# Half of the w_out projection set into attention, its norm split in two, and the norm between two blocks done by row tile

## The reference

```
first block:
  proj = rmsnorm(x) @ w_in                       # 1024 x 2560, cut into q, k, v, u, vg
  sb   = stick_breaking_attention(q, k, v)       # 8 heads of 64, causal
  sg   = gelu(u) * (W_spatial . rmsnorm(gelu(vg)) + b)      # "gated" unit, 512 wide
  h    = x + concat(rmsnorm(sb), rmsnorm(sg)) @ w_out       # 1024 x 1024
  h    = h + moe(rmsnorm(h))     # 4 groups x 8 experts of width 512, 2 experts per token
  y    = rmsnorm(h) * g_final
second block:
  z    = rmsnorm(y) @ w_in_2 + b                 # 1024 x 7168
  u    = causal depthwise convolution, 31 taps (conv_a), layer norm, silu, product
  v    = short convolution, RG-LRU scan, product; gated sum; projection w_o
  x    = y + m @ w_o; x = x + relu(rmsnorm(x) @ w_1)^2 @ w_2;  rmsnorm
```

## Time and profile before

| what | value |
|---|---|
| time, median of 3 runs | 1077.96 us (1077.39 to 1079.14) |
| the profiled execution's own time | 1080.09 us |
| its span | 1078.6 us |
| TensorE busy | 896.8 us (83%) |
| VectorE busy | 526.9 us (49%) |
| ScalarE busy | 344.6 us (32%) |
| POOL busy | 133.4 us (12%) |
| DMA, mean over the span | 278 GB/s, 299.98 MB |
| the chain that ended last | PE 52%, DMA 29%, DVE 14%, ACT 2% |

### The profile page before, as it was taken

The page is one execution under the profiler, slowest core; times in us unless marked ns, Lnnn a source line. Parts: engine busy times, 40 slices in busy tenths (PEclk is TensorE's granted clock), DMA queues, the critical chain, the costliest instruction groups (busy, mean ns, idle before and its releaser), DMA issues.

```text
span 1078.6 us, 18062 instructions
## 1 busy us (share of the span) xinstructions
PE 896.8 (83%) x7891; PEld 724.1 (67%) x7891; DVE 526.9 (49%) x845; ACT 344.6 (32%) x463; POOL 133.4 (12%) x67
## 2 busy tenths in 40 slices
PE   8998988966475746475565899999999989999997
PEld 8987875533243424242342599689999989988986
DVE  4644554222131212112021769999997857635542
ACT  5624221100000001000000734557756446443531
POOL 1032400000000000000001288603210000000000
PEclk9998999888787868778688899999999999999999
DMA  9870748999999999999999645325568444546420
GB/s 343 260 300 2 300 168 371 426 426 427 426 428 428 428 428 430 428 428 430 428 428 420 198 162 191 117 93 171 168 211 283 173 170 166 207 157 218 173 78 39
DMA packets 86727, 299.98 MB, mean 278 GB/s; under 512 B 12381, under 2 KB 50701, under 8 KB 74253
## 3 DMA queue, kind: packets, MB, share of 16 engines
q1 hardware_dynamic: 86525, 299.13, 70.7%
q10 hardware_dynamic: 144, 0.00, 0.0%
HBM read 298.07 MB, written 1.05 MB: 277 GB/s over the span
## 4 chain that ended last, share of the span: by engine, by line
PE 52%; DMA 29%; DVE 14%; ACT 2%; issue 2%; SPq 1%; DVEq 0%
DMA mem<-in_w_up 25%; PE PS L1772 12%; PE PS L1773 12%; PE PS L1774 12%; PE PS L1954 8%; DVE PS L1547 6%; PE PS L1967 3%; DMA mem<-in_w_down 3%; DMA mem<-in_w_in 1%; DVE PS L1572 1%; PE PS L1940 1%; DMA mem<-in_w 1%; PE PS L1980 1%; PE PS L1746 1%; DVE PS L1568 1%
## 5 line engine op out<-in xcount | busy, mean ns | idle before, releaser
L1954 PE MATMUL PS<-mem 128*32 128x256 f32 x2048 | 156.6, 473 | 136.0 <-DMA mem<-in_w_up 135.4
L1954 PEld LDWEIGHTS PS<-mem 128*32 128x32 f32 x2048 | 83.6, 136 | 210.6 <-issue 184.6
L1774 PE MATMUL PS<-HT_hi,ring_rest 128*128 128x256 f32 x752 | 212.8, 283 | 0.0
L1774 PEld LDWEIGHTS PS<-HT_hi,ring_rest 128*128 128x128 f32 x752 | 143.9, 191 | 0.0
L1328 DVE TENSOR_TENSOR mem<-mem,PS 128x128 f32<-128x128 f32 x32 | 12.1, 379 | 261.2 <-ACT mem L809 261.2
L1772 PE MATMUL PS<-HT_hi,z_hi 128*128 128x256 f32 x440 | 124.9, 284 | 2.3 <-DVE ring_rest L1522 2.3
L1773 PE MATMUL PS<-HT_rest,z_hi 128*128 128x256 f32 x440 | 124.5, 283 | 0.0
L653 POOL TENSOR_TENSOR ring_rest<-mem,z_hi 128x2048 fp32r<-128x2048 f32 x19 | 87.6, 4622 | 95.1 <-DVE ring_rest L1522 55.9
L1685 DVE TENSOR_TENSOR ring_rest<-mem,mlp_hi 128x4096 fp32r<-128x4096 f32 x16 | 70.8, 4424 | 57.7 <-ACT mlp_hi L1027 57.7
L809 ACT ACTIVATE mem<-PS 128x128 f32<-128x128 f32 x32 | 8.9, 278 | 272.3 <-PE PS L1954 272.3
L1547 DVE SCALAR_TENSOR_TENSOR PS<-mem,CAW,PS 128x256 f32<-128x256 f32 x232 | 91.3, 480 | 0.0
(11 more groups left out here) (357 smaller groups left out, 1817.7 us busy)
## 6 DMA issues: line engine op xcount, KB each, us to landing
mem<-in_w_gate SPq DMA_DIRECT2D x32, 2048.0 KB, 16.5
mem<-in_w_up SPq DMA_DIRECT2D x32, 2048.0 KB, 20.9
mem<-in_w_down SPq DMA_DIRECT2D x31, 2048.0 KB, 12.7
mem<-in_w SPq DMA_DIRECT2D x16, 2048.0 KB, 8.1
mem<-in_w_in SPq DMA_DIRECT2D x30, 1024.0 KB, 5.3
mem<-in_w_in SPq DMA_DIRECT2D x4, 2048.0 KB, 18.3
mem<-in_w_b_out SPq DMA_DIRECT2D x4, 1536.0 KB, 8.9
mem<-in_w_out SPq DMA_DIRECT2D x2, 2048.0 KB, 14.7
```

The lines of the kernel that those rows point to most:

```text
L1774: ins = nc.tensor.matmul(dst, s_rest, m_hi, start=False, stop=stop and n == len(terms) - 1, skip_group_check=True)
L1954: ins = nc.tensor.matmul(PS[SLOTS * j:SLOTS * (j + 1), bank, 0:2 * F_STRIP].rearrange("p (w n) -> p w n", w=2), xg[:, k, :], w[:, :, k, F_ ...
```

## The change

Four things are edited.

- The projection's channels are ordered anew: w_out is loaded as two DMAs per block, and the first half of the chunks holds attention's channels, the second the gated unit's. The products of one column half and one channel half (`out1_product(n, half)`) are 24 matmuls. The gated half's products of column half 2 stand before the last `weighted_values`, those of 3, 0 and 1 after it, and attention's half of all four follows. `out1_ps` counts the latter alone.
- High parts of w_out are made by ScalarE, in the order 2, 3, 0 before the first `att_log` and 1 after the second; the remainders of 2 and 3 by POOL, of 0 and 1 by VectorE. The high parts of 2 and 3 lie in slot 3, so w_down of expert 1 is loaded after w_down of expert 0.
- The norm of the w_out input is split: the gated part's squares, factor (by Ln and Exp with one correction step on VectorE instead of a root and a reciprocal), rows, turning, gains and splits stand between the third pair's weights and the fourth pair's softplus. Attention's part stays behind the fourth pair. The turning of the tables for the second block moves ahead of attention, and the keep-busy matmuls around the old turning go.
- Between the blocks, squares, gain and scaling go tile by tile; POOL's first remainder waits for both rows; the scalings that keep the first block's output in X move behind the remainder of the second half; the first two products are done together, high x high of both first (`first_pair`).

```diff
         out1_hi = [parts(f"out1_hi{n}", mem_at + 4 * at, KC, HALF)
-                   for n, at in enumerate((4 * SLOT_FLOATS, 4 * SLOT_FLOATS + HALF_FLOATS, a0 + D, a0 + D + HALF_FLOATS))]
+                   for n, at in enumerate((4 * SLOT_FLOATS, 4 * SLOT_FLOATS + HALF_FLOATS, 3 * SLOT_FLOATS, 3 * SLOT_FLOATS + HALF_FLOATS))]
...
+        MIX_QUARTERS = [(tt, slice(KC // 2 * half, KC // 2 * (half + 1))) for half in (1, 0) for tt in range(TT)]
+        OUT1_SPLIT = (2, 3, 0, 1)
+
+        def out1_place(n, tt):
+            return PS[:, (6 if n < 2 else 0) + tt, (n % 2) * HALF:(n % 2 + 1) * HALF]
...
+                if n >= IN1_BLOCKS:
+                    b = n - IN1_BLOCKS
+                    for half in range(2):
+                        ks = slice(KC // 2 * half, KC // 2 * (half + 1))
+                        sp.dma_start(chunked(n % RING, BLOCK)[:, ks, :], w_out1[half][:, :, b * BLOCK:(b + 1) * BLOCK]).then_inc(loaded[n % RING], 16)
+                    continue
+                w, b = w_in1, IN1_ORDER[n]
...
             load_gate_up(1, first)
-            sp.wait_ge(*in1_used(7))
-            load_down(1, *first[2])
             sp.wait_ge(rows, rows_before["ffn"])
             sp.wait_ge(tables_turned, 1)
             load_gate_up(THIRD_EXPERT, third)
...
             sp.wait_ge(out1_ps, 8)
             load_down(0, *second[2])
+            load_down(1, *first[2])
...
-            for n in range(4):
+            for n in OUT1_SPLIT[:2]:
                 raw, rest = out1_half(n)
...
+                pool.wait_ge(out1_hi_ready, OUT1_SPLIT.index(n) + 1)
+                for k in range(0, KC, KC // 4):
+                    at = slice(k, k + KC // 4)
                     ins = nc.gpsimd.tensor_tensor(rest[:, at, :], raw[:, at, :], out1_hi[n][:, at, :].bitcast(F32), ALU.subtract)
                 ins.then_inc(out1_rest_ready, 1)
...
             pool.wait_ge(z_hi_ready, 1)
+            pool.wait_ge(rows, rows_before["mix2"] + TT)
...
-            pool.wait_ge(rows, rows_before["mix2"] + TT)
...
+            def mix_factor(col, rows_, *ready):
+                for tt in range(TT):
+                    act.wait_ge(*ready[tt])
+                    add_squares(rows_[tt], col + tt, square[:, 0:SB])
+                link(nc.scalar.activation(rstd[:, col:col + TT], ss[:, col:col + TT], ACT.Ln, scale=1.0 / SB, bias=eps[:, :]))
+                nc.scalar.activation(rstd[:, col:col + TT], rstd[:, col:col + TT], ACT.Exp, scale=-0.5).then_inc(rms_ready, 1)
+
+            def split_out1(n):
+                w = IN1_BLOCKS + n // 2
+                if n % 2 == 0:
+                    act.wait_ge(*in1_used(7 if n == 2 else IN1_HALVES - 1))
+                    act.wait_ge(loaded[w % RING], out1_count(w))
+                nc.scalar.activation(out1_hi[n][:, :, :], out1_half(n)[0], ACT.Copy).then_inc(out1_hi_ready, 1)
+
...
+            for n in OUT1_SPLIT[:3]:
+                split_out1(n)
             att_log(0)
...
             act.wait_ge(tables_turned, 1)
...
+            att_log(1)
+            split_out1(OUT1_SPLIT[3])
+            att_weights(0)
+            att_log(2)
+            att_weights(1)
+            mix_factor(6, [so[:, tt, :] for tt in range(TT)], (so_ready, 1), (so_ready, 2))
+            att_weights(2)
+            att_log(3)
+            split_hT("mix", range(TT))
+            att_weights(3)
+            mix_factor(4, [PS[:, 2 + tt, :] for tt in range(TT)], (av_done, PAIRS), (av_done, PAIRS))
+            split_hT("mix", range(TT, 2 * TT))
...
             att_softplus(1)
             att_masked(0)
             att_masked(1)
+            gating(0)
             att_softplus(2)
-            gating(0)
+            gating(1)
             att_masked(2)
+
+            def mix_rows(name, half, col, src):
+                dve.wait_ge(rms_ready, rms_order.index(name) + 1)
+                sums, factor, part, step = ss[:, col:col + TT], rstd[:, col:col + TT], ss[:, 10:12], ss[:, 12:14]
+                link(nc.vector.tensor_scalar(part, sums, -0.5 / SB, -0.5 * EPS, ALU.mult, ALU.add))
+                link(nc.vector.tensor_tensor(step, factor, factor, ALU.mult))
+                link(nc.vector.tensor_tensor(step, step, part, ALU.mult))
+                link(nc.vector.scalar_tensor_tensor(factor, step, 1.5, factor, ALU.add, ALU.mult))
+                for tt in range(TT):
+                    to = HN[:, tt, KC // 2 * half:KC // 2 * (half + 1), :].rearrange("p k q -> p q k")
+                    nc.vector.tensor_scalar(to, src[tt].rearrange("p (q k) -> p q k", k=KC // 2), rstd[:, col + tt:col + tt + 1], None,
+                                            ALU.mult).then_inc(rows, 1)
+
+            mix_rows("mix gated", 1, 6, [so[:, tt, :] for tt in range(TT)])
+            apply_gain("mix", G_MIX, range(TT))
             att_softplus(3)
-            gating(1)
+            rest_hT("mix", range(TT))
             att_masked(3)
...
+            for n in OUT1_SPLIT[2:]:
+                raw, rest = out1_half(n)
+                dve.wait_ge(out1_hi_ready, OUT1_SPLIT.index(n) + 1)
+                dve.wait_ge(out1_rest_ready, OUT1_SPLIT.index(n))
+                nc.vector.tensor_tensor(rest, raw, out1_hi[n][:, :, :].bitcast(F32), ALU.subtract).then_inc(out1_rest_ready, 1)
+            mix_rows("mix", 0, 4, [PS[:, 2 + tt, :] for tt in range(TT)])
+            apply_gain("mix", G_MIX, range(TT, 2 * TT))
+            rest_hT("mix", range(TT, 2 * TT))
...
+            def square_terms(tt):
                 dve.wait_ge(first_squares, tt + 1)
                 nc.vector.tensor_scalar(ss[:, 8 + tt:9 + tt], ss[:, 10 + tt:11 + tt], EPS / D, EPS * EPS, ALU.mult,
                                         ALU.add).then_inc(mix2_in, 1)
+
+            for tt in range(TT):
+                for n in (2 * tt, 2 * tt + 1):
+                    add_part(PACKS - 1, n)
+                    if n == 2:
+                        square_terms(0)
                 dve.wait_ge(comb_free, 4 * (PACKS - 1) + 2 + 2 * tt + 2)
                 nc.vector.tensor_tensor(HG[:, tt, :], X[:, tt, :], g_first[:, :], ALU.mult).then_inc(gained, 1)
             for tt in range(TT):
                 dve.wait_ge(rms_ready, rms_order.index("mix2") + tt + 1)
                 link(nc.vector.reciprocal(rstd[:, 12 + tt:13 + tt], rstd[:, 12 + tt:13 + tt]))
+                if tt == 0:
+                    square_terms(1)
                 nc.vector.tensor_scalar(permuted(tt), plain(HG[:, tt, :]), rstd[:, 12 + tt:13 + tt], None, ALU.mult).then_inc(rows, 1)
...
             rest_half(1)
+            inverse_rms("first", 10, TT)
+            for tt in range(TT):
+                nc.vector.tensor_scalar(X[:, tt, :], HG[:, tt, :], rstd[:, 10 + tt:11 + tt], None, ALU.mult)
...
+                keep_busy(3, 3)
...
+            def turn_mix(half, n0):
+                for tt in range(TT):
+                    pe.wait_ge(rows, TT + n0 + tt + 1)
+                    if n0 > 0:
+                        pe.wait_ge(hT_ready, hT_count("mix", n0 - TT + tt))
+                    for k in range(KC // 2):
+                        ins = nc.tensor.transpose(PS[:, 4 + tt, k * P:(k + 1) * P], HN[:, tt, KC // 2 * half + k, :], ident[:, :])
+                    ins.then_inc(turned, 1)
+
+            def out1_product(n, half):
+                pe.wait_ge(out1_rest_ready, OUT1_SPLIT.index(n) + 1)
+                for tt in range(TT):
+                    terms = rows_times(tt, out1_hi[n][:, :, :], out1_half(n)[1])[KC // 2 * half:KC // 2 * (half + 1)]
+                    ins = three_passes(out1_place(n, tt), terms, half == 1 and n % 2 == 0, half == 0)
+                    if half == 0:
+                        ins.then_inc(out1_ps, 1)
+
+            later_keys(1)
+            scores(2)
+            spatial_mixing(1)
             pe.wait_ge(tables_ready, 3)
+            weighted_values(0)
+            later_keys(2)
+            scores(3)
+            weighted_values(1)
+            turn_mix(1, 0)
+            later_keys(3)
+            weighted_values(2)
+            pe.wait_ge(hT_rest_ready, split_count("mix", TT - 1))
+            out1_product(2, 1)
+            weighted_values(3)
+            out1_product(3, 1)
+            out1_product(0, 1)
+            turn_mix(0, TT)
+            out1_product(1, 1)
+            pe.wait_ge(hT_rest_ready, split_count("mix", 2 * TT - 1))
             for n in range(4):
...
+                out1_product(n, 0)
...
+            def first_pair(hi, rest):
+                cols = [slice(i * P, (i + 1) * P) for i in range(2)]
+                pe.wait_ge(hT_hi_ready, split_count("mix2", 3))
+                for i in range(2):
+                    for k in range(KC):
+                        nc.tensor.matmul(by_token_tile(PS[:, i, 0:T]), hi[:, k, cols[i]], HT_hi[:, :, k, :], start=k == 0, stop=False,
+                                         skip_group_check=True)
+                pe.wait_ge(z_rest_ready, 1)
+                for i in range(2):
+                    for k in range(KC):
```

(34 more changed lines are left out.)

95 lines of the change are left out of this document (29 added, 66 removed).

## The result

The changed kernel takes 1066.22 us (median of 4 runs, 1064.48 to 1068.51) against 1077.81 for the kernel before on the same chip: a ratio of 0.989, 95% interval 0.987 to 0.992. Forecast were 1065.5 and 1058.5 to 1072.5. Run again later, it took 1066.48 (6 runs). The profiled execution has 1067.41 us and a span of 1065.7; the forecast for a profile like that of before was 1067.6.

What follows compares the result with a forecast made beforehand. TensorE's chain of attention, projection and router, then a fixed 432 us of DMA, was taken as the bound. Gains of 9.7 + 2.8 = 12.5 us took the profile from 1080.1 to 1067.6, so 1065.5 at the median; range 1058.5 to 1072.5.

Steps and rivals of the forecast that it cites:

- Bound and passing on: From expert 3's w_gate issue the stage ends about 432 us after `gu_done` 1; bringing that forward shifts its end equally.
- High parts, remainders, gated norm at 0: In attention, w_out's high parts and VectorE's remainders cost 0; gated-norm insertions find idle engines, `later_keys(3)` comes at 97.65.
- the clock term: In attention and projection, TensorE at 1.2 GHz from about 99.6 to 109.8 us, costing 4.7 us.
- Full-clock end: At 2.4 GHz the projection ends at 126.1 us instead of 140.5, 14.4 us earlier; `gu_done` 1 at 149.5.
- a rival, with 6 us left of the 14.4: Attention: clock falls already in the third pair, or insertions delay the fourth softplus 3 us; 1070 us; chance 0.13.
- The projection's term, 9.7: Projection by w_out: 14.4 us gained at full clock, less 4.7 us at half speed, leaves 9.7 us.
- The norm (2.8 us): Norm between the blocks: products of z end 2.1 to 4.6 us earlier, capped at about 3.8; 2.8 taken.
- the cap of 3.8: Before conv_a: X scalings waiting for POOL subtractions let conv_a start at 626 to 628, limiting the norm's gain.
- POOL beside VectorE: Behind the norm, POOL's remainder meets the `HT_rest` subtractions, and each X scaling can wait for a 4.6 us subtraction.
- The stall of TensorE for the remainder: After the high-times-high products of z, TensorE waits 0 to 1.5 us for POOL's remainder; 0.5 taken.
- the sum 12.5: Whole kernel: 9.7 us from the projection plus 2.8 us from the norm.
- the held clock: Attention: TensorE's clock holds through the third and fourth pairs; gain 18 us, time 1060; chance 0.15.

Runs made afterwards that it cites:

- fill: The changed kernel with three more keep-busy matmuls of TensorE in attention, one before later_keys of the third pair, two before the fourth's: 1064.35 us.
- proj_only: The changed kernel with the norm between the blocks as before, so the projection part alone: 1066.87 us, ratio 0.9913.
- best: The changed kernel with three more keep-busy matmuls in attention and the two scalings of X on ScalarE: 1063.30 us, ratio 0.986.
- before_fill: The kernel before with four 128x512 fillers on TensorE between the second norm's transposes and the first product of z: 1079.78 us, ratio 1.0022.
- best_fill: `best` with four fillers more ahead of the first product of z and four ahead of the MLP's: 1065.32 us, ratio 0.9875.
- after_again: The changed kernel once more, unedited, on another chip: 1066.48 us.
- z_early: The changed kernel with POOL's first remainder of z started once its high part is there, not after the norm's scalings: 1067.12 us.

## Why the prediction was right, step by step

- **Bound and passing on: right.** Issue to last landing was taken as 432 us and fixed; it is 431.4 to 432.0 in twelve profiles of thirteen. The queue was nearly empty around the issue (0.13 of the DMA in 150 to 155 us), w_down of expert 1 stayed hidden. That VectorE is 99% busy from conv_a on holds in the kernel before to 760 us; behind that TensorE is the full one (89.87 of 90 us to 850). The gain was passed on through both.
- **High parts, remainders, gated norm at 0: right.** ScalarE's copies and VectorE's remainders (4.68 us for the two, from 104.01) lie in waits. With a full clock ahead of it `later_keys(3)` comes at 97.71 (`fill`) and 97.56 (`proj_only`); 97.65 was worked out. In the changed kernel's first profile it came at 100.07, which is the clock's doing (see the clock term).
- **Full-clock end: right.** The issue was put at 149.5; `fill` has 149.51, and one profile of the changed kernel 149.54. (The keep-busy matmuls that go with the old turning are fourteen in the trace, from seven calls, not eight.)
- **The clock term (4.7 us lost): its size met by luck in the first profile, too large on average, and the wrong shape.** One fall of 10 us from 99.6 was assumed. The first profile lost 4.5 in another way: 0.8 ahead of attention, most of the rest by two falls of about 3.4 us, the first already in the third pair (0.60 from 90 to 94). Four of the six profiles with the new projection and no filler fell in the third pair; the prediction had that as a rival, with 6 us left of the 14.4, but it cost 2.8 to 4.6 in all, since the fourth pair's fall was mostly short. Over all six the loss against 149.5 is 0 to 4.6: the issues average 152.5, so 3.0 are lost. And the old order falls too, more in some runs (169.16) than in the profile from which the sum was made. The projection's term, 9.7, measured 11.1 by the medians; the ratio's 7.2 to 11.6 holds both.
- **The norm (2.8 us): met in the two profiles compared, too large as a worth.** In them it is 2.8. As a change by itself it measured 1.8 (at most 2.6 by the interval), and 0.5 to 0.8 on top of the projection by the medians. The step that failed is taking the long low clock of the earlier trace rows as given: in `proj_only` the same code has it for 3.4 us instead of 10 and is 2.2 us faster. The working had the pair of products end 2.1 to 4.6 us earlier; it was 3.9 in the profile, and the X scalings gave 1.1 of it back, as the cap of 3.8 had said in kind.
- **POOL beside VectorE: right in kind.** The stall of TensorE for the remainder is 0.84 us (0.5 was taken), HT_rest doubled. The Trainium skill (SBUF — State Buffer, "SBUF: two separate sides") has the engine that starts first hold the shared port pair for its whole instruction, where VectorE's has two SBUF inputs or runs in a 2-port mode. The trace agrees for the scalings of X, if they run in that mode, which no run here shows: each is as long as one of POOL's 4.6 us subtractions and a bit (10.18 for two). HT_rest's four pieces beside POOL's quarter-size pieces took twice their time, 4.97 for 2.49.
- By the medians two errors of opposite sign, 1.4 too little and 1.0 to 2.3 too much, made the sum 12.5 where 11.6 and 12.0 were measured. That they cancel is luck; the intervals leave the first one open. Of the rivals, the held clock came nearest: in one of two profiles it fell for some 3.4 us only, and the issue was at 149.54; the span was 1064.7 all the same, since a fall further on took 2.8 us back (from w_o to the chain's MLP load 104.3 us instead of 101.5).

What stays open: why the clock is 0.57 at 12 us in some executions and 1.00 in others of one program. It put the first wait of attention's chain 0.8 us later (71.34 instead of 70.54), and no kernel here aims at it. Open too is what the old order of the norm costs with the clock held.

## What to carry to other kernels

Work that doesn't depend on the critical norm belongs in front of it as soon as its inputs exist: 96 products (11.5 us) moved ahead of it, and the keep-busy matmuls behind them dropped, brought the issue forward by 12.1 us on average, and the stage behind passed all of it on. Fillers seem to pay where they fit the gap and begin at a high clock (issue at 149.51 and 149.29 in `fill` and `best`, which had a full clock at 12 us; the changed kernel managed 149.54 once without them); longer than the gap or behind a fall they were slow work in the way (`before_fill`, and in front of the MLP `best_fill`). A term that one profile's clock explains is a range: the issue alone moved by 4.4 us between two profiles of one program.

## What the runs showed of the hardware

- The granted clock differs between executions of one program, at the same places. The two profiles of the changed kernel have 0.57 and 1.00 at 12 us, 0.60 and 1.00 from 90 to 94, and in front of the MLP one stays at 1.00 where the other has 0.57 from 872 to 880. In attention, at the norm and in front of the MLP a wait of TensorE of 1.4 to 2.8 us stands ahead, after transposes or narrow products; but the same wait is not always followed by a fall (1.69 us in front of the MLP's first product in `best`, with the clock at 1.00 from 866 to 880).
- What it costs: 0.8 us at 12 us, up to 4.5 in attention (issue at 149.5 to 154.0 in profiles with a full clock at 12 us), 1.5 to 2.8 in front of the MLP (103.0 and 104.3 us from w_o to the chain's MLP load in `fill` and `after_again`, 101.5 in nine of thirteen profiles). That this makes the spread of 4 to 5 us between runs that are otherwise alike is likely, but not shown: only the profiled executions have a trace.
- Two `tensor_scalar` of 128x1024 on VectorE took 1.42 us in POOL's pause and 10.18 beside its 128x2048 subtractions. POOL's four 128x512 pieces and HT_rest's four beside them took 7.05 us together (597.59 to 604.64). An estimate for one after the other is 7.1: 4.6 for POOL, four quarters of its 4.62 us subtraction, and 2.49 for HT_rest without POOL (`z_early`).
- Four 128x512 fillers of fp32 are eight matmuls in the trace and took 3.67 us at the full clock, not the 1.7 of the estimate.
